# A two-layer hybrid decoder step: key rotation through summed products, earlier lora loads, and new orders in the scan loop and the output projection

## The chip, the cores and the metric

The kernel runs on one core of a Trainium2 chip. Its metric is the device time of one execution in microseconds (us), the median of several runs. The core's engines are TensorE (PE, matrix products into PSUM banks), VectorE (DVE), ScalarE (ACT), GpSimd (POOL) and SyncE (SP, which only issues transfers here). Each engine runs its own list of instructions in the order in which it is written; engines meet only at semaphores.

## The reference

Two groups of tokens share the weights: a prompt of 1024 positions and 8 samples of one position each, so every stage works on T = 1032 columns. Each of two layers does:

```python
h = rmsnorm(x, W['attn_norm'][l])
proj = h @ W['w_in'][l]                       # 1024 -> 2592
q, k = rope(q, positions), rope(k, positions)  # 8 query heads, 2 key heads of 64
yb = swa_banded(q, k, v, sink)                 # or swa_step for the samples: window of 128, learned sinks
w = -softplus(-(w0 + tanh(wlo) @ w_decay_up)) - 0.5 ; decay = exp(-exp(w))
a = sigmoid(a0 + alo @ w_a_up) ; g = sigmoid(glo) @ w_g_up
S = S * decay + (S @ -kk) (kk*a)^T + v k_mod^T ; y = S r     # RWKV-7 scan over 1024 steps
ya = (groupnorm(y) + bonus) * g
x = x + concat(ya, yb) @ W['w_out'][l]
x = x + (silu(h2 @ w_gate) * (h2 @ w_up)) @ w_down,  h2 = rmsnorm(x, ffn_norm)
```

`rope` turns each pair of halves of a head by an angle that grows with the position: x1 cos - x2 sin, x2 cos + x1 sin. All of it is float32, and the states, shifted rows and key and value windows of both groups are outputs too.

## The kernel before, in words

Activations lie features by tokens: 128 features on the partitions, 1032 tokens as three column groups of 344 (`NC3`, `CW`). A projection's weights come in units of 128 x 1024; the products keep float32 accuracy by splitting weight and activation into a high and a low part and summing three matmuls (`column`, L1597 to L1599). So each unit passes three engines ahead of PE: SP loads it (`fill_dma`, L383), ACT rounds it to the high part (`fill_high`, L578), POOL subtracts to get the low part (`fill_low`, L491). There are three slots for units, dealt out by `slot`. One unit and one column group take 24 matmuls, which the text calls a column.

Per layer the stages follow one another: the in-projection; the rotation; windowed attention; attention of the samples; the two loras, decay, and norm of the scan's keys; the scan in 16 chunks of 64 tokens; the output projection `w_out` with the samples' scan step beside it; and the FFN. In the profiled execution layer 0 has them from about 26, 279, 312, 405, 434, 560, 718 and 862 us on, layer 1 begins at 1605 us.

**Rotation.** DVE and PE handle four pairs of query heads, each by column group: PE multiplies by a matrix that swaps the halves (L1632), DVE multiplies the product by the sine table (L1035), the projection by the cosine table (L1036), and adds (L1038); the next pair's product waits for that sum. Then come the keys: for each of two heads and three column groups PE makes two products, of the key rows doubled (L1638) and of the key rows doubled and swapped (L1639), and DVE multiplies and adds them (L1044, L1045, L1047) into `a_k_twice`. Attention's first product (L1674) waits for the last of these.

**Loads.** SP issues the rope tables, mask and windows when the in-projection leaves their memory, and the weights of decay and a (`wda`) and the scan mask (`smask`) after the samples' attention is done (L427, L428). PE's lora product (L1761) waits for both.

**Chunk loop.** Chunk n hands its output, two chunks to a block m of 128 tokens, to a norm over heads: the tables `CENTRE_AT`, `SQUARE_AT` and `NORM_AT` (L317 to L319) say in which chunk block m is centred, squared (ACT, L789), given its root (ACT `y_root`, L794) and normed (DVE, L1289); `tokens_back` (PE, L1904) turns it back. In the first chunks DVE also finishes an elimination for the second half of the chunks (`FIRST`, L1308) and lays out its result (`blocks_out`, `corner_out`) in chunk 5; PE's state product (L1927) waits for DVE's state (L1348).

**w_out.** PE runs columns of the first two column groups, then eight of the third; between them stand the products of the samples' scan step (`dec_sums` L1983 and L1985, `dec_read` L1991, and the norm at L2025 to L2031). Activation blocks 0 to 3 are split here (`out_high` on ACT, L798; `out_low` on POOL, L534), blocks 4 to 7 come back by transfer (L540). `add_out` (DVE, L1431) adds a column to the residual.

**Into the FFN.** While PE runs the third column group, ACT squares the residual, and DVE and ACT make the normed activation's high and low parts of the first two groups (`normed` L1445, `high2` L874, `low2` L1450); the table `NORMED` (L321) says how many of the 16 pairs follow each column. The FFN's first gate product waits for them, and the next for the silu (L883).

## Time and profile before

| what | value |
|---|---|
| median of 3 runs | 3250.84 us (3250.83, 3260.38, 3250.84) |
| profiled execution | 3248.73 us, span 3246.8 us, mean granted clock of PE 0.933 |
| busy PE | 2916.8 us, 90% of the span |
| busy DVE, ACT, POOL | 1461.5, 824.1, 606.3 us |
| chain that ended last | PE 75%, DVE 16%, ACT 4%, issue 3%, DMA 1% |

The page says for each engine how long it worked, and for the chain that ended last which engine held up the end. PE is busy nine tenths of the span, so what can be gained lies in the remaining 330 us, in which PE waits, and in stretches in which its granted clock is half. A row of a timeline gives the start, the duration, the engine, the line, the tile written and those read, and in brackets the idle time before it and what ended that. A row of windows gives busy times in a stretch, then the granted clock (1.00 is 2.4 GHz, 0.50 is 1.2 GHz), the DMA share and the rate.

### The profile page before, as it was taken

To read this page: it belongs to the slowest core of one execution; us is meant where nothing else is said; L and a number is where in the kernel's file an instruction comes from. 1 tells how busy PE (TensorE), PEld (TensorE's weight loads), DVE (VectorE), ACT (ScalarE), POOL (GpSimd) and SP (SyncE) were. 2 spreads that over 40 slices of the span, in tenths; PEclk is the share of its full clock that TensorE was granted. 3 is DMA by queue.
4 is the path that set the end of the run, shared out by engine and by line. 5 is a ranking of instruction groups with operands and counts; after the bars stand their busy time and mean duration, and the time that the engine had idled before them with its cause. 6 is when DMAs were issued, how large, how long until landed. Compare 5 with 4: busy or idle time off the path is not lost.

```text
span 3246.8 us, 49233 instructions
## 1 busy us (share of the span) xinstructions
PE 2916.8 (90%) x20858; PEld 2741.4 (84%) x20858; DVE 1461.5 (45%) x2549; ACT 824.1 (25%) x1727; POOL 606.3 (19%) x295
## 2 busy tenths in 40 slices
PE   6996766988899999999999966589898999999997
PEld 6995635878899999999989946368788999999997
DVE  5334749765622322223453275687645322223324
ACT  3000642441311111111310035424323111111112
POOL 2320001013222122222222100000232222222123
PEclk9998966989999999999999988669899999999998
DMA  3111010023211111111211010000322111111111
GB/s 120 46 33 52 1 40 11 15 67 106 65 55 49 40 52 46 46 46 46 81 58 51 15 52 12 29 11 15 111 84 62 46 40 53 47 51 46 40 53 53
DMA packets 55882, 158.13 MB, mean 49 GB/s; under 512 B 9200, under 2 KB 23536, under 8 KB 54896
## 3 DMA queue, kind: packets, MB, share of 16 engines
q1 hardware_dynamic: 52496, 150.76, 14.8%
q0 software_dynamic: 3168, 4.23, 0.5%
q8 instruction: 166, 2.72, 0.3%
q14 instruction: 52, 0.43, 0.0%
HBM read 137.43 MB, written 17.54 MB: 48 GB/s over the span
## 4 chain that ended last, share of the span: by engine, by line
PE 75%; DVE 16%; ACT 4%; issue 3%; DMA 1%; SPq 0%; POOL 0%; DVEq 0%; ACTq 0%
PE bank L1597 21%; PE bank L1599 20%; PE bank L1598 20%; PE bank L1962 1%; PE bank L1958 1%; PE bank L1938 1%; DVE a_stats L1092 1%; PE bank L1819 1%; PE bank L1853 1%; PE bank L1948 1%; PE bank L1761 1%; DVE act_low L964 1%; DVE c_T L1217 1%; PE bank L1665 1%; DVE c_NT L1215 1%
## 5 line engine op out<-in xcount | busy, mean ns | idle before, releaser
L1597 PE MATMUL bank<-act_high,w_high 128*128 128x344 f32 x3504 | 1139.2, 325 | 49.8 <-POOL w_low L491 34.6
L1599 PE MATMUL bank<-act_high,w_low 128*128 128x344 f32 x3504 | 1129.3, 322 | 0.0
L1598 PE MATMUL bank<-act_low,w_high 128*128 128x344 f32 x3504 | 1129.1, 322 | 0.0
L491 POOL TENSOR_TENSOR w_low<-w_raw,w_high 128x1024 fp32r<-128x1024 f32 x206 | 522.0, 2540 | 1677.0 <-ACT w_high L578 1661.1
L1597 PEld LDWEIGHTS bank<-act_high,w_high 128*128 128x128 f32 x3504 | 668.0, 191 | 59.0 <-POOL w_low L491 39.5
L1598 PEld LDWEIGHTS bank<-act_low,w_high 128*128 128x128 f32 x3504 | 666.3, 190 | 2.6 <-issue 2.1
L1599 PEld LDWEIGHTS bank<-act_high,w_low 128*128 128x128 f32 x3504 | 667.5, 191 | 0.0
L1460 DVE TENSOR_TENSOR f_mid<-f_silu,bank 128x344 f32<-128x344 f32 x132 | 67.7, 513 | 852.9 <-PE bank L1599 849.6
L1557 DVE TENSOR_TENSOR resid<-bank,resid 128x344 f32<-128x344 f32 x528 | 270.6, 516 | 209.5 <-PE bank L1599 209.5
L1597 PE MATMUL bank<-f_mid_high,w_high 128*128 128x344 f32 x1056 | 341.8, 324 | 4.1 <-DVE resid L1557 4.0
L1599 PE MATMUL bank<-f_mid_high,w_low 128*128 128x344 f32 x1056 | 339.6, 322 | 0.0
L1598 PE MATMUL bank<-f_mid_low,w_high 128*128 128x344 f32 x1056 | 337.3, 319 | 0.0
L578 ACT CAST w_high<-w_raw 128x1024 fp32r<-128x1024 f32 x206 | 212.5, 1043 | 489.9 <-PE bank L1599 487.0
L1597 PEld LDWEIGHTS bank<-f_mid_high,w_high 128*128 128x128 f32 x1056 | 198.4, 188 | 10.6 <-DVE resid L1557 10.1
L1599 PEld LDWEIGHTS bank<-f_mid_high,w_low 128*128 128x128 f32 x1056 | 198.8, 188 | 0.0
L1598 PEld LDWEIGHTS bank<-f_mid_low,w_high 128*128 128x128 f32 x1056 | 198.5, 188 | 0.2
L1013 DVE TENSOR_TENSOR proj<-bank,s_rstd 128x344 f32<-128x344 f32 x126 | 64.3, 516 | 292.0 <-PE bank L1599 291.9
L890 ACT CAST f_mid_high<-f_mid 128x344 fp32r<-128x344 f32 x132 | 63.5, 481 | 406.7 <-DVE f_mid L1460 406.7
L883 ACT ACTIVATE f_silu<-bank 128x344 f32<-128x344 f32 x132 | 60.2, 458 | 351.7 <-PE bank L1599 351.7
L628 ACT COPY s_raw_last<-proj 128x9 f32<-128x9 f32 x30 | 6.0, 200 | 279.8 <-DVE proj L1013 279.8
L1254 DVE TENSOR_TENSOR c_gram<-bank,consts 128x512 f32<-128x512 f32 x64 | 41.2, 686 | 69.5 <-PE bank L1819 69.2
L1702 PEld LDWEIGHTS bank<-a_probs_t,a_v_padded 128*128 128x128 f32 x512 | 60.0, 196 | 14.6 <-DVE a_probs_t L1075 10.7
(287 smaller groups left out, 3010.3 us busy)
## 6 DMA issues: line engine op xcount, KB each, us to landing
w_raw<-wts SPq DMA_DIRECT2D x206, 512.0 KB, 3.6
resid<-x SPq DMA_DIRECT2D x4, 1376.0 KB, 10.5
att_keep<-act_low SPq DMA_DIRECT2D x2, 2064.0 KB, 10.2
act_low<-att_keep POOLq DMA_DIRECT2D x6, 688.0 KB, 4.6
x_keep<-resid SPq DMA_DIRECT2D x3, 1376.0 KB, 5.8
o_y<-resid SPq DMA_DIRECT2D x3, 1376.0 KB, 5.7
resid<-x SPq DMA_DIRECT2D x4, 516.0 KB, 7.7
...
```

Source lines behind the costliest of these rows:

```text
L491: eng.tensor_tensor(wl[s][:, :], raw[s][:, :], wh[s][:, :].bitcast(F32), ALU.subtract).then_inc(w_low, 1)
L578: eng.copy(wh[s][:, :], raw[s][:, :]).then_inc(w_high, 1)
L883: a(sil[:, c, :], bank[c][:, 0:CW], ACT.Silu).then_inc(scalar_steps, e.step(f"ff{i}_sil{j}{c}"))
L890: eng.copy(mh[:, j, cs(c)], midf[:, c, :]).then_inc(scalar_steps, e.step(f"ff{i}_high{j}{c}"))
L1013: tt(proj[:, k, cs(c)], bank[3 * (k % 2) + c][:, 0:CW], rstd[:, c, :], ALU.mult).then_inc(vector_steps, e.step(f"win_ev{k}{c}"))
L1254: tt(GM[n % 2][:, h], bank[h][:, :].rearrange("p (k t) -> p k t", k=4), bcast(c_("gram"), 1, 4), ALU.mult).then_inc(vector_steps, e.step(f ...
L1460: tt(midf[:, c, :], sil[:, c, :], bank[3 + c][:, 0:CW], ALU.mult).then_inc(vector_steps, e.step(f"ff{i}_mid{j}{c}"))
L1557: tt(x[:, k, cs(c)], bank[(DOWN_LAST if i == NR - 1 else DOWN)[n % (4 if i == NR - 1 else 2)]][:, 0:CW], x[:, k, cs(c)], ALU.add).then_inc ...
L1597: mm(out, wh[s][:, wcols], act_h, start=start, stop=False)
L1598: mm(out, wh[s][:, wcols], act_l, start=False, stop=False)
L1599: return mm(out, wl[s][:, wcols], act_h, start=False, stop=stop)
L1702: last = mm(bank[6][:, 128 * p:128 * p + 128], v, pT[:, 2 * (2 * p + h) + kt, :], start=(h, kt) == (0, 0), stop=(h, kt) == (1, 1))
```

## The change

Five parts, all in both layers. **Keys:** DVE first multiplies the key rows by cosine and by sine (128 x 1032 each); PE makes both products into one bank, where they are summed (`key_heads`), head 0 after the first query pair and head 1 after the second; ACT copies the six sums to `a_k_twice`. **Loads:** `wda` and `smask` are issued directly behind the value window, and the tiles that share their memory are moved. **Chunk loop:** the centre, square and norm of the first four blocks come one chunk later, the elimination's steps are dealt out anew, its layout is spread over chunks 5 to 7, and the root of block 6 is taken ahead of chunk 15's copy. **w_out:** the first column comes before the samples' sums, the samples' steps come a column or two later, and the first units are loaded and split earlier than the second group's activations. **Into the FFN:** ACT splits the next unit before it squares, `NORMED` deals out the pairs differently with five after the loop, and the second silu comes before the first high part.

```diff
-CENTRE_AT = {6: 0, 7: 1, 8: 2, 9: 3, 11: 4, 12: 5, 14: 6}
-SQUARE_AT = {7: 0, 8: 1, 9: 2, 10: 3, 12: 4, 13: 5, 15: 6}
-NORM_AT = {8: 0, 9: 1, 10: 2, 11: 3, 13: 4, 14: 5}
+CENTRE_AT = {7: 0, 8: 1, 9: 2, 10: 3, 11: 4, 12: 5, 14: 6}
+SQUARE_AT = {8: 0, 9: 1, 10: 2, 11: 3, 12: 4, 13: 5, 15: 6}
+NORM_AT = {9: 0, 10: 1, 11: 2, 12: 3, 13: 4, 14: 5}
-NORMED = (0, 3, 5, 7, 9, 12, 14, 16)
+NORMED = (0, 2, 4, 6, 8, 9, 10, 11)
...
+eng.dma_start(wda, row("wda").rearrange("p (w n) -> p w n", w=2)).then_inc(lora_in, e.load("lora_in"))
+eng.dma_start(smask[:, :], d["smask"]).then_inc(lora_in, e.load("lora_in", "lora_in"))
...
 if l:
     eng.wait_ge(spill, e.at("spill"))
-eng.wait_ge(tensor_steps, e.at(f"y{NCH - 1}"))
+eng.wait_ge(tensor_steps, e.at(f"y{NCH - 2}"))
 eng.sem_inc(sync_idle, 1)
 fill_dma(l, NIN, wait=False)
...
     eng.dma_start(hl[:, 4:8, cs(c)], kept_low[:, :, cs(c)]).then_inc(att_back[c], e.load(f"att_back{c}", f"att_back{c}"))
-    if c < 2:
+    if c == 0:
         for o in range(4):
             out_low(c, o)
 eng.sem_inc(pool_idle, 1)
 fill_low(l, NIN)
+for o in range(4):
+    out_low(1, o)
+eng.wait_ge(vector_steps, e.at("y_n7"))
+fill_low(l, NIN + 1)
 eng.wait_ge(tensor_steps, e.at("yt7"))
-fill_low(l, NIN + 1)
 fill_low(l, NIN + 2)
 for k in range(NIN + 3, UL + 3 if l < L - 1 else UL):
     fill_low(l, k)
-    if k == NIN + 7:
+    if k == NIN + 8:
         for o in range(4):
             out_low(2, o)
...
+eng.wait_ge(pool_steps, e.at("att_zero"))
 for g in range(2):
-    eng.wait_ge(vector_steps, e.at("kd_last"))
+    for c in range(NC3):
+        eng.wait_ge(tensor_steps, e.at(f"rk{g}{c}"))
+        eng.copy(kd[:, g, WIN + c * CW:WIN + (c + 1) * CW], bank[3 + c][:, 0:CW]).then_inc(scalar_steps, e.step(f"kd{g}{c}"))
+for g in range(2):
...
+    if n == NCH - 1:
+        y_root(SQUARE_AT[n])
...
 
-y_square(7)
 eng.wait_ge(vector_steps, e.at("y_gated5"))
+fill_high(l, NIN)
 for o in range(4):
     out_high(1, o)
-fill_high(l, NIN)
+y_square(7)
+eng.wait_ge(state_out, e.at("state_out"))
+fill_high(l, NIN + 1)
 y_root(7)
...
     fill_high(l, NIN + 3 + k, used=f"wo_mm{k}1")
-    if k == 3:
+    if k == 4:
         eng.wait_ge(tensor_steps, e.at("dn_var"))
         a(drs[:, 0:32], bank[2][:, 64:96], ACT.Sqrt, bias=eps_lnx, scale=1.0 / HD).then_inc(scalar_steps, e.step("dn_root"))
-    if k == 4:
+    if k == 5:
         eng.wait_ge(vector_steps, e.at("dn_out"))
         for o in range(4):
...
+    fill_high(l, NIN + KT + 3 + k, used=f"wo_mm{k}2")
     square(k, 2)
-    fill_high(l, NIN + KT + 3 + k, used=f"wo_mm{k}2")
     if k == 0:
         root("n2", 0)
         root("n2", 1)
     else:
         for i in range(NORMED[k - 1], NORMED[k]):
             high2(i // KT, i % KT)
+for i in range(NORMED[-1], 2 * KT):
+    high2(i // KT, i % KT)
 silu(0, 0, 0)
 root("n2", 2)
 for k in range(KT):
     high2(2, k)
+silu(0, 0, 1)
 mid_high(0, 0, 0)
 silu(0, 1, 0)
-silu(0, 0, 1)
 mid_high(0, 0, 1)
 silu(0, 1, 1)
 silu(0, 0, 2)
...
 eng.sem_inc(vector_idle, 1)
+tt(kcos[:, :], proj[:, 19, :], cos[:, :], ALU.mult).then_inc(vector_steps, e.step("k_cos"))
+tt(ksin[:, :], proj[:, 19, :], sin[:, :], ALU.mult).then_inc(vector_steps, e.step("k_sin"))
...
-for g in range(2):
-    for c in range(NC3):
-        kt = kd[:, g, WIN + c * CW:WIN + (c + 1) * CW]
-        eng.wait_ge(tensor_steps, e.at(f"rk{g}{c}"))
-        eng.wait_ge(vector_steps, e.mine())
-        tt(rt[:, c, :], bank[3 + c][:, 0:CW], sin[:, cs(c)], ALU.mult).then_inc(vector_steps, e.step())
-        tt(kt, bank[c][:, 0:CW], cos[:, cs(c)], ALU.mult).then_inc(vector_steps, e.step())
-        eng.wait_ge(vector_steps, e.mine())
-        tt(kt, kt, rt[:, c, :], ALU.add).then_inc(vector_steps, e.step("kd_last" if (g, c) == (1, 2) else f"kd{g}{c}"))
 
...
-FIRST = (0, 0, 5, 8, 13, 16, 21, 24, 29, 31)
+FIRST = (0, 0, 5, 9, 12, 15, 19, 22, 27, 31)
 grams(0)
...
-        for h in range(2):
-            blocks_out(1, h, 1)
-            corner_out(1, h)
+        blocks_out(1, 0, 1)
+    elif n < 8:
+        corner_out(1, 0) if n == 6 else blocks_out(1, 0, 0)
     if n + 1 < NCH:
...
     elif n == 5:
-        for h in range(2):
-            blocks_out(1, h, 0)
+        blocks_out(1, 1, 1)
+    elif n < 8:
+        corner_out(1, 1) if n == 6 else blocks_out(1, 1, 0)
     if n in NORM_AT:
...
+for i in range(NORMED[-1], 2 * KT):
+    if i + 1 < 2 * KT:
+        normed((i + 1) // KT, (i + 1) % KT)
+    low2(i // KT, i % KT)
 inverse("n2", 2)
...
 eng.wait_ge(vector_steps, e.at(f"win_ev{NIN - 1}2"))
+def key_heads(g):
+
+    eng.wait_ge(vector_steps, e.at("k_sin"))
+    for c in range(NC3):
+        if g:
+            eng.wait_ge(scalar_steps, e.at(f"kd0{c}"))
+        mm(bank[3 + c][:, 0:CW], dup[:, 128 * g:128 * g + 128], kcos[:, cs(c)], start=True, stop=False)
+        mm(bank[3 + c][:, 0:CW], rdup[:, 128 * g:128 * g + 128], ksin[:, cs(c)], start=False, stop=True).then_inc(tensor_steps, e.step(f"rk{g}{c}"))
+
 for p in range(4):
+    if p in (1, 2):
+        key_heads(p - 1)
     for c in range(NC3):
         if p:
             eng.wait_ge(vector_steps, e.at(f"rq_add{p - 1}{c}"))
         mm(bank[c][:, 0:CW], rotm, proj[:, 15 + p, cs(c)], start=True, stop=True).then_inc(tensor_steps, e.step(f"rq_rot{p}{c}"))
+eng.wait_ge(scalar_steps, e.at("kd12"))
 eng.wait_ge(vector_steps, e.at("rq_add32"))
-for g in range(2):
-    for c in range(NC3):
-        if g:
-            eng.wait_ge(vector_steps, e.at(f"kd0{c}"))
-        mm(bank[c][:, 0:CW], dup[:, 128 * g:128 * g + 128], proj[:, 19, cs(c)], start=True, stop=True)
-        mm(bank[3 + c][:, 0:CW], rdup[:, 128 * g:128 * g + 128], proj[:, 19, cs(c)], start=True, stop=True).then_inc(tensor_steps, e.step(f"rk{g}{c}"))
-eng.wait_ge(vector_steps, e.at("kd_last"))
 eng.wait_ge(pool_steps, e.at("att_zero"))
...
+out_column(0, 0)
+eng.wait_ge(vector_steps, e.at("y_gated6"))
+tokens_back(7)
 eng.wait_ge(vector_steps, e.at(f"S_new{NCH - 1}"))
 eng.wait_ge(scalar_steps, e.at(f"y_ev{NCH - 1}"))
 dec_sums(0, 0)
-out_column(0, 0)
 dec_sums(0, 1)
-eng.wait_ge(vector_steps, e.at("y_gated6"))
-tokens_back(7)
 out_column(0, 1)
 out_column(1, 0)
+out_column(1, 1)
 dec_read(0)
-out_column(1, 1)
+out_column(2, 0)
 dec_sums(1, 0)
 dec_sums(1, 1)
-out_column(2, 0)
 out_column(2, 1)
+out_column(3, 0)
 dec_read(1)
-out_column(3, 0)
+out_column(3, 1)
+out_column(4, 0)
 eng.wait_ge(vector_steps, e.at("y_gated7"))
 eng.wait_ge(vector_steps, e.at("dec_y11"))
 mm(bank[2][:, 0:32], c_("centre"), dy[:, :], start=True, stop=True).then_inc(tensor_steps, e.step("dn_centred"))
 eng.wait_ge(vector_steps, e.at("dn_r_k_k"))
 mm(bank[2][:, 32:64], bdones, dbp[:, :], start=True, stop=True).then_inc(tensor_steps, e.step("dn_bonus"))
-out_column(3, 1)
+out_column(4, 1)
+out_column(5, 0)
 eng.wait_ge(vector_steps, e.at("dn_squares"))
 eng.wait_ge(vector_steps, e.at("dn_bonus_v"))
 mm(bank[2][:, 64:96], bdones, dsq[:, :], start=True, stop=True).then_inc(tensor_steps, e.step("dn_var"))
-for k in range(4, KT):
+out_column(5, 1)
+for k in range(6, KT):
     out_column(k, 0)
     out_column(k, 1)
 out_column(0, 2)
```

The order of the samples' steps on DVE (from `y_variance(7)` on) follows PE's: column sums come one place earlier, `dec_y`, `dec_squares` and `dec_out` a place or two later.

**Order of instructions.** PE at the rotation of layer 0 before: twelve products of the query pairs, then the keys; `a_rope_mats` holds the matrices, `proj` the projected rows.

```order
1515 L1632 MATMUL bank<-proj,a_rope_mats 128x344 x12
1516 L1638 MATMUL bank<-proj,a_rope_mats 128x344
1517 L1639 MATMUL bank<-proj,a_rope_mats 128x344
1518 L1638 MATMUL bank<-proj,a_rope_mats 128x344
1519 L1639 MATMUL bank<-proj,a_rope_mats 128x344
```

And in the changed kernel, where a piece of three is one query pair:

```order
1515 L1652 MATMUL bank<-proj,a_rope_mats 128x344 x3
1516 L1643 MATMUL bank<-a_k_cos,a_rope_mats 128x344
1517 L1644 MATMUL bank<-a_k_sin,a_rope_mats 128x344
1518 L1643 MATMUL bank<-a_k_cos,a_rope_mats 128x344
...
1522 L1652 MATMUL bank<-proj,a_rope_mats 128x344 x3
1523 L1643 MATMUL bank<-a_k_cos,a_rope_mats 128x344
1524 L1644 MATMUL bank<-a_k_sin,a_rope_mats 128x344
...
1529 L1652 MATMUL bank<-proj,a_rope_mats 128x344 x6
```

The twelve key products moved from behind the query pairs to between them, and read DVE's scaled copies.

POOL at the end of the chunk loop of layer 0 before; a row x4 is `out_low` of one column group, L540 a transfer from `att_keep`, and L491 a unit's low part, from `w_out`'s first on.

```order
41 L540 DMA act_low<-att_keep 128x4x344
42 L534 TENSOR_TENSOR act_low<-proj,act_high 128x344 x4
43 L540 DMA act_low<-att_keep 128x4x344
44 L534 TENSOR_TENSOR act_low<-proj,act_high 128x344 x4
45 L540 DMA act_low<-att_keep 128x4x344
46 L491 TENSOR_TENSOR w_low_63<-w_raw_57,w_high_60 128x1024
47 L491 TENSOR_TENSOR w_low_64<-w_raw_58,w_high_61 128x1024
```

The same place in the changed kernel:

```order
41 L542 DMA act_low<-att_keep 128x4x344
42 L536 TENSOR_TENSOR act_low<-proj,act_high 128x344 x4
43 L542 DMA act_low<-att_keep 128x4x344 x2
44 L493 TENSOR_TENSOR w_low_62<-w_raw_56,w_high_59 128x1024
45 L536 TENSOR_TENSOR act_low<-proj,act_high 128x344 x4
46 L493 TENSOR_TENSOR w_low_63<-w_raw_57,w_high_60 128x1024
47 L493 TENSOR_TENSOR w_low_64<-w_raw_58,w_high_61 128x1024
```

The first unit's low part now stands ahead of the second group's `out_low`.

PE at the start of `w_out` in layer 0 before: `tokens_back` (L1904), the samples' sums on `d_t_a` and `d_t_b`, and the first column's products (L1597 to L1599).

```order
1970 L1904 MATMUL bank<-consts,y_normed_151 128x128 x4
1971 L1983 MATMUL bank<-d_t_a,consts 128x512
1972 L1985 MATMUL bank<-d_t_a,consts 128x512
1973 L1597 MATMUL bank<-act_high,w_high_60 128x344
1974 L1598 MATMUL bank<-act_low,w_high_60 128x344
...
1996 L1599 MATMUL bank<-act_high,w_low_63 128x344
1997 L1983 MATMUL bank<-d_t_b,consts 128x512
1998 L1985 MATMUL bank<-d_t_b,consts 128x512
1999 L1904 MATMUL bank<-consts,y_normed_152 128x128 x4
2000 L1597 MATMUL bank<-act_high,w_high_60 128x344
```

In the changed kernel:

```order
1972 L1918 MATMUL bank<-consts,y_normed_153 128x128 x4
1973 L1606 MATMUL bank<-act_high,w_high_59 128x344
1974 L1607 MATMUL bank<-act_low,w_high_59 128x344
...
1996 L1608 MATMUL bank<-act_high,w_low_62 128x344
1997 L1918 MATMUL bank<-consts,y_normed_154 128x128 x4
1998 L1997 MATMUL bank<-d_t_a,consts 128x512
1999 L1999 MATMUL bank<-d_t_a,consts 128x512
2000 L1997 MATMUL bank<-d_t_b,consts 128x512
2001 L1999 MATMUL bank<-d_t_b,consts 128x512
2002 L1606 MATMUL bank<-act_high,w_high_59 128x344
```

The first column now follows `tokens_back(6)` at once, and both sums stand behind it and behind `tokens_back(7)`.

## Rows read from the trace of the kernel before

**Rows 1.** Page, groups: count, busy us, mean ns, idle before <-releaser.
```profile
L1597 PE MATMUL bank<-act_high,w_high 128*128 128x344 f32 x3504 | 1139.2, 325 | 49.8 <-POOL w_low L491 34.6
L578 ACT CAST w_high<-w_raw 128x1024 fp32r<-128x1024 f32 x206 | 212.5, 1043 | 489.9 <-PE bank L1599 487.0
```

**Rows 2.** Timeline, PE, layer 0: start us, duration us, [idle before <-releaser].
```profile
279.25 4.04 PE L1632 MATMUL bank<-proj,a_rope_mats 128*128 128x344 f32 x8 [7.83 <-DMA a_amask<-amask]
306.81 0.74 PE L1638 MATMUL bank<-proj,a_rope_mats 128*128 128x344 f32 x2
307.39 0.74 PE L1639 MATMUL bank<-proj,a_rope_mats 128*128 128x344 f32 x2
311.72 0.49 PE L1674 MATMUL bank<-a_k_twice,proj 64*128 64x256 f32 x2 [3.58 <-DVE a_k_twice L1047]
```

**Rows 3.** Timeline of DVE in the same stretch, first and last of 36 instructions.
```profile
280.88 0.52 DVE L1035 TENSOR_TENSOR a_rope_tmp<-bank,a_sin 128x344 f32<-128x344 f32 x1 [7.76 <-PE bank L1632]
298.63 0.52 DVE L1038 TENSOR_TENSOR proj<-proj,a_rope_tmp 128x344 f32<-128x344 f32 x1
```

**Rows 4.** Windows: stretch, busy us of PE PEld DVE ACT POOL, clock, DMA.
```profile
284.00:296.00 12.00, 6.71 (x16) 2.32 (x16) 11.48 (x24) 0.00 (x0) 0.00 (x0) 1.00 0.00 0
1888.00:1900.00 12.00, 8.91 (x14) 4.02 (x14) 8.87 (x19) 0.00 (x0) 0.00 (x0) 0.50 0.00 0
```

**Rows 5.** Instructions of one line, 128x1032 products on DVE.
```profile
L1178 DVE TENSOR_TENSOR proj<-proj,e_a_term x8: 1210/1226/1234, 467.1 to 2093.3; 128x1032 f32<-128x1032 f32 x8
```

**Rows 6.** Timeline of PE and ACT, start of the decay stage, layer 0.
```profile
433.96 3.79 PE L1761 MATMUL bank<-proj,e_w_decay_a 64*128 64x512 f32 x8 [6.67 <-DMA e_scan_mask<-smask]
...
427.41 1.06 ACT L704 ACTIVATE proj<-proj 64x1032 f32<-64x1032 f32 x1
```

**Rows 7.** DMA issues while the rope tables load: KB, median us to landing.
```profile
a_v_window<-vwin SPq DMA_DIRECT2D x1, 508.0 KB, 8.1
a_amask<-amask SPq DMA_DIRECT2D x1, 256.0 KB, 6.0
```

**Rows 8.** Timeline of PE, chunk loop of layer 0.
```profile
621.46 0.68 PE L1927 MATMUL bank<-c_S,ar_heads 64*64 64x64 f32 x16 [1.38 <-DVE c_S L1348]
...
642.11 1.07 PE L1938 MATMUL bank<-c_SA,c_Tt 64*64 64x64 f32 x16 [1.16 <-ACT c_SA L812]
```

**Rows 9.** Windows of the chunk loop, layer 0 and layer 1.
```profile
643.00:657.00 14.00, 14.00 (x143) 12.19 (x141) 5.63 (x13) 4.13 (x12) 0.00 (x0) 0.54 0.01 2
2250.00:2262.00 12.00, 11.88 (x189) 10.52 (x190) 8.70 (x19) 6.27 (x18) 0.00 (x0) 1.00 0.00 1
```

**Rows 10.** Timeline of PE, w_out of layer 0.
```profile
721.60 0.69 PE L1904 MATMUL bank<-consts,y_normed 128*128 128x128 f32 x2 [3.48 <-DVE y_normed L1289]
...
724.65 1.19 PE L1983 MATMUL bank<-d_t_a,consts 128*128 128x512 f32 x1 [1.94 <-ACT act_high L798]
...
732.39 0.66 PE L1597 MATMUL bank<-act_high,w_high 128*128 128x344 f32 x1 [3.99 <-POOL w_low L491]
...
775.86 0.38 PE L2025 MATMUL bank<-d_y,consts 128*128 128x32 f32 x2 [3.91 <-DVE d_y L1395]
...
783.59 0.38 PE L2031 MATMUL bank<-d_squares,consts 128*128 128x32 f32 x2 [1.73 <-DVE d_bonus L1411]
```

**Rows 11.** Timeline of ACT at the end of the chunk loop.
```profile
718.15 0.58 ACT L829 COPY y_tokens<-bank 64x512 f32<-64x512 f32 x1 [3.19 <-PE bank L1962]
```

**Rows 12.** Window from w_out's third column to the FFN, layer 0.
```profile
822.00:886.00 64.00, 51.91 (x300) 49.77 (x299) 50.54 (x69) 27.31 (x49) 18.69 (x8) 0.95 0.23 73
```

**Rows 13.** Timeline of PE in the same stretch.
```profile
843.13 0.43 PE L1597 MATMUL bank<-act_high,w_high 128*128 128x344 f32 x1 [2.05 <-POOL w_low L491]
...
849.22 0.42 PE L1597 MATMUL bank<-act_high,w_high 128*128 128x344 f32 x1 [2.05 <-POOL w_low L491]
```

**Rows 14.** Timeline of POOL and of DVE there, one fill.
```profile
827.55 2.40 POOL L491 TENSOR_TENSOR w_low<-w_raw,w_high 128x1024 fp32r<-128x1024 f32 x1 [3.42 <-ACT w_high L578]
...
827.88 2.43 DVE L1450 TENSOR_TENSOR act_low<-n_normed,act_high 128x344 fp32r<-128x344 f32 x1 [1.39 <-ACT act_high L874]
```

More of the change, by code:

```diff
@@ L238, in program @@
         rt = sp("rope_tmp", 3 * CW)[:, :].rearrange("p (c t) -> p c t", c=3)
+        kcos, ksin = (at(f"a_k_{n}", T, RING + 7152 - T * (i + 1)) for i, n in enumerate(("cos", "sin")))
         kro = sp("k_tail", 136)
@@ L289, in program @@
         SA0 = at("c_SA0", 256, RING + 3584)[:, :].rearrange("p (k t) -> p k t", k=4)
-        St = [at(f"c_S{q}", 256, RING + 3840 + 256 * q)[:, :].rearrange("p (k t) -> p k t", k=4) for q in range(2)]
+        St = [at(f"c_S{q}", 256, RING + 4352 - 256 * q)[:, :].rearrange("p (k t) -> p k t", k=4) for q in range(2)]
         elim = [at(f"c_N{f}", 1024, RING + 4608 + 2304 * f) for f in range(2)]
@@ L298, in program @@
         heads_of = lambda v: v.rearrange("p (g i) -> p g i", g=8)
-        yt = [at(f"y_tokens{m}", 512, (PJ + 12 * T + 512 * m, RING + 4608, RING + 7168)[max(m - 2, 0)]) for m in range(5)]
+        yt = [at(f"y_tokens{m}", 512, (PJ + 12 * T + 512 * m, RING + 4608, RING + 6144)[max(m - 2, 0)]) for m in range(5)]
         bv = [at(f"y_bonus_v{m}", 512, (PJ + 12 * T + 1536 + 512 * m, RING + 5120, RING + 5632)[max(m - 2, 0)]) for m in range(5)]
-        lgr = at("y_ln_gain", 512, RING + 6144)
-        ysq = at("y_squares", 512, RING + 6656)
+        lgr = at("y_ln_gain", 512, RING + 7168)
+        ysq = at("y_squares", 512, RING + 7680)
         yn = [at(f"y_normed{q}", 512, RING + 8192 + 512 * q) for q in range(2)]
@@ L348, in program @@
         w_low = sem("w_low_ready")
-        PER_SLOT = (34, 35, 34)
+        PER_SLOT = (35, 34, 34)
         def slot(k):
-            return (k + 2) % 3 if k < NIN else (k - NIN + 1) % 3
+            return (k + 1) % 3 if k < NIN else (k - NIN) % 3
         def unit_of(l, k):
@@ L426, in _ @@
                 eng.wait_ge(k_out, e.at("k_out"))
-                eng.dma_start(wda, row("wda").rearrange("p (w n) -> p w n", w=2)).then_inc(lora_in, e.load("lora_in"))
-                eng.dma_start(smask[:, :], d["smask"]).then_inc(lora_in, e.load("lora_in", "lora_in"))
                 eng.dma_start(d["att_keep"].rearrange("p (k t) -> p k t", k=4).bitcast(F32), hl[:, 4:8, :].bitcast(F32)).then_inc(att_out, e.load("att_out", "att_out"))
@@ L832, in _ @@
                         corner(n + 2, 1, 0)
-                    if n in SQUARE_AT:
+                    if n in SQUARE_AT and n < NCH - 1:
                         y_root(SQUARE_AT[n])
@@ L1473, in _ @@
                 y_variance(7)
+                y_norm(7)
                 dec_in(0, 1)
-                y_norm(7)
+                y_gate(7)
+                add_out(0, 0)
                 dec_back(0, 0)
-                y_gate(7)
                 dec_back(0, 1)
-                add_out(0, 0)
+                add_out(0, 1)
                 dec_state(0)
-                add_out(0, 1)
                 add_out(1, 0)
+                add_out(1, 1)
                 dec_y(0)
+                sum2(1, 0)
                 dec_in(1, 0)
-                add_out(1, 1)
-                sum2(1, 0)
+                add_out(2, 0)
+                sum2(1, 1)
                 dec_in(1, 1)
@@ L1489, in _ @@
                 dec_back(1, 1)
-                add_out(2, 0)
-                sum2(1, 1)
-                dec_state(1)
                 add_out(2, 1)
                 sum2(2, 0)
+                dec_state(1)
                 add_out(3, 0)
```

27 lines of the change are left out of this document (12 added, 15 removed).

## The prediction

> **What bounds the kernel now.** I read the page's groups first, then PE's timeline of each stage that the diff touches, then the windows of those stages. The table of the profile shows PE busy for 2916.8 of 3246.8 us; what the change can give lies in the 330 us without a matmul and in stretches at half clock. The groups say where weights are late: the first of each three products waited 49.8 us in all, 34.6 of it for POOL's low part, while ACT's rounding of a unit takes 1.04 us [rows 1]. The timelines then show that the five edited places hold waits of other kinds: DVE's chain in the rotation, a transfer ahead of the lora product, single stalls in the chunk loop, and in `w_out` and behind it a supply chain of ACT, POOL and DVE. I go through them in the order of a layer, count layer 0 and double it, since layer 1 has the same waits.
>
> **Rotation.** Before, PE may start at 279.25, when the mask has landed [rows 2], and DVE's 36 instructions for the queries run from 280.88 to 298.63 + 0.52 = 299.15 [rows 3], 18.27 us without a gap. Only then come the keys; attention starts at 311.72 [rows 2]. So the keys cost 311.72 - 299.15 = 12.6 us of pure path. After, DVE first makes two products of 128 x 1032. A row of that shape and operation has a median of 1.226 us [rows 5], so they last from 279.35 to 281.8; the queries' chain starts 281.8 - 280.88 = 0.9 us later than before and, if PE keeps up, ends at 300.1. PE gets 6 key products behind the first pair and 6 behind the second. At full clock one follows the next after 307.39 - 306.81 = 0.58 us [rows 2], so six take 3.5 us, against 18.27 / 4 = 4.57 us that DVE spends on a pair: hidden. At half clock six take 7.0 us and DVE waits. The first six start at about 281.8, just behind a DMA wait of 7.83 us [rows 2], and will be cold in part; I give that 1.0 us, so attention starts at about 301.2 and the term is 311.7 - 301.2 = **10.5 us**. ACT's six copies hide behind the third and fourth pair, since ACT has nothing else there (0.00 busy in both windows [rows 4]). Bounds: 11.5 us with no cold product; at half clock all the way PE needs 24 products x 1.16 = 27.8 us from 279.25, and one DVE step of 1.5 us behind, 308.6, which leaves 3.1 us.
>
> **Loads of the lora stage.** PE's product at 433.96 stood 6.67 us for the scan mask; the other thing it needs, ACT's tanh, was done at 427.41 + 1.06 = 428.47 [rows 6]. With the transfers issued some 150 us earlier the tanh is last, and the gain is 433.96 - 428.47 = **5.5 us**. What is moved: two transfers go into the burst of the rope tables. They stand behind the value window in SP's queue, and in this burst what was issued first landed first: the mask after 6.0 us, the value window after 8.1 [rows 7]. So I charge the rotation nothing. If the engines mixed them, two more transfers, each like a window, would delay the mask by up to the 2.1 us between those rows; the term is then 3.4. The Trainium skill ("DMA: Bandwidth & Descriptors", section "Two DMAs through the same engine are not ordered") says that nothing orders transfers across the sixteen engines, which speaks for that lower figure; the landing times of this trace stand against it, without excluding it.
>
> **Chunk loop.** One stall goes with the spread of the elimination's layout: 1.38 us on DVE's state at 621.46 [rows 8]. The other, 1.16 us at 642.11 behind ACT, belongs to the first root and moves a chunk on. The new tables move work between chunks but add none. I take **1.3 us**, bounds 5 (layer 0's half-clock stretch behind 642.11 disappears, below) and -5 (another one appears).
>
> **w_out.** Up to the first column PE waited 3.48 + 1.94 + 3.99 = 9.41 us, and for the samples' norm 3.91 + 1.73 = 5.64 [rows 10]; these five are 15.05 us per layer. After: the loop's last matmul ends at 721.60 - 3.48 = 718.12. ACT's last copy ends at 718.15 + 0.58 = 718.73 [rows 11]; the first unit has been loaded a chunk earlier and is now rounded at once, 1.04 us, to 719.8, and POOL's part takes 2.40 [rows 14], to 722.2. `tokens_back(6)` (724.65 - 1.94 - 721.60 = 1.1 us [rows 10]) fits before that, as block 6's root no longer waits for that copy. So the first column starts at 722.2 and not at 732.39; of 4.1 us, 1.1 are work and 3.0 are waiting: 9.4 - 3.0 = **6.4 us**. `dec_sums` then stands behind the column, where ACT's and DVE's steps have passed. What is queued behind POOL's fill now is the second group's `out_low`; its column comes after two sums and `tokens_back(7)`, at about 733, and the low part is ready at 722.2 + 5.3 = 727.5. For the samples' norm a column or two more stand ahead of each wait. The row at 849.22 less its wait of 2.05, minus 843.13, gives 4.0 us for a column [rows 13], enough for 3.91 and 1.73 if DVE's chain ran unchanged; but additions to the residual now stand ahead of it, so I take three quarters, **4.1 us**. Together **10.5**; bounds 13 (all but the 3.0, and the first column warm) and 5 (the norm's waits stay).
>
> **Into the FFN.** From 822 to 886 PE works 51.91 of 64 us [rows 12]: 12.1 us of waits, two of them of 2.05 us on POOL at 843.13 and 849.22 [rows 13]. ACT now rounds the next unit before it squares, so POOL starts earlier; five pairs are left until after the loop and then stand ahead of the silu. I take half, **6 us**, bounds 11 and 0. Against more speaks a row: DVE's subtraction `low2` beside POOL's fill took 2.43 us, where an operation of that size takes 0.52 elsewhere, and they ended one just behind the other, at 829.95 and 830.31 [rows 3, 14]. The Trainium skill ("SBUF — State Buffer", "Who interferes with whom") has a rule for this: a VectorE operation with two inputs in SBUF and a GpSimd operation that reads SBUF exclude one another for the whole instruction. The rows agree. By it a fill may cost DVE 1.9 us at each of eight columns however the pairs are dealt out, and this term is nothing; the second rival prices that.
>
> **Sum.** 10.5 + 5.5 + 1.3 + 10.5 + 6 = 33.8 us per layer, 67.6 in two. The profiled execution took 3248.7 us and comes to 3181; the median of the runs lies 2.1 us above it, so I say 3183.
>
> **Rivals.**
> First, the rotation is bound by PE at half clock. For it: in layer 1 the clock is 0.50 from 1888 to 1900, though in layer 0 the same work ran at 1.00 from 284 to 296 [rows 4], and the change begins with a wait for DVE. Against: PE has twice the work between the pairs. The term is 3.1 in place of 10.5, 15 us in two layers: 3198.
> Second, supply stays the bound: DVE and POOL exclude one another as above. `w_out` gives 5 and the FFN's start 0, so 2 x 11.5 = 23 us are missing: 3206. For it: the subtraction of 2.43 us [rows 14]. Against: the first column's 6.4 us do not depend on it.
> Third, supply comes free: the FFN's start gives 11 and `w_out` 12.5, 2 x 7 = 14 us more: 3169.
> Fourth, slower: the reordered chunk loop lets PE fall to half clock. The price: behind the stall of 1.16 us [rows 8] layer 0 ran 143 instructions in 14.0 us at 0.54; in layer 1 a stretch of the same loop took 12 us for 189 at 1.00 [rows 9]. Each such stretch costs 14.0 x (1 - (12.0 / 189) / (14.0 / 143)) = 4.9 us. It decides from (67.6 + 10) / 4.9 = 16 stretches on, one in half of the 32 chunks: 3260 and more. Against: the tables remove a stall and create no longer one that I can see, and layer 1 kept its clock.
>
> **How the numbers follow.** Forecast 0.52, first rival 0.13, second 0.16, third 0.12, fourth 0.07. A measurement of this kernel tells about 0.3% from no change, 10 us; all cases but the fourth lie beyond it. Of the fourth I put 0.04 beyond 3260 and 0.02 within 10 us of before. So: faster 0.94, same 0.02, slower 0.04. The range: at the low end third rival with the rotation at its bound, 2 x (11.5 + 5.5 + 3 + 12.5 + 11) = 87, 3164, and a little for the clock: 3158. At the high end the second rival with the first in one layer, 3206 + 7 = 3213, rounded down to 3212, since both at once are rare.
>
> **What would show it.** The rotation: attention's first product about 21.9 us after the first query product, not 32.5, and no DVE instruction on `a_k_twice`. Loads: the lora product released by ACT, not by DMA. Chunk loop: no stall over a microsecond on `c_S`. `w_out`: its first column 4 to 5 us after the loop's last matmul, and no wait near 4 us on POOL or `d_y`. FFN's start: waits of 6 us instead of 12 from the third columns to the first silu. Wrong it would be if the granted clock in the rotation or the loop is 0.50 for most of the stage, or if the third columns keep a period above 6 us.

## The result and the profile after

The changed kernel takes 3167.41 us (median of 4 runs, 3166.18 to 3170.12), the kernel before 3253.82 (4 runs, 3250.83 to 3260.38): a ratio of 0.9733, 95% interval 0.9715 to 0.9751. The profiled execution took 3167.29 us, 81.4 less than that of before, with a mean granted clock of 0.945 instead of 0.933. The forecast was 3183, so the direction was right and the gain larger than its sum. The page's head and its first group after:

```profile
span 3165.3 us, 49209 instructions
PE 2885.1 (91%) x20858; PEld 2722.5 (86%) x20858; DVE 1453.9 (46%) x2517; ACT 830.3 (26%) x1739; POOL 613.3 (19%) x295
L1606 PE MATMUL bank<-act_high,w_high 128*128 128x344 f32 x3504 | 1134.7, 324 | 42.5 <-POOL w_low L493 24.3
```

PE is busy 31.7 us less for the same 20858 matmuls: that part of the gain is not waiting, but matmuls of which fewer run at half clock. The group answers to [rows 1]: 10.3 us less wait on POOL's low part.

Where it went, as differences between two starts on PE's timeline, kernel before minus kernel after:

| stage | forecast per layer | layer 0 | layer 1 |
|---|---|---|---|
| first query product to attention's first | 10.5 | 9.8 | 10.0 |
| to the lora product | 5.5 | 4.1 | 3.8 |
| to the loop's first products with the state | 0 | -1.5 | 0.0 |
| to the loop's last matmul | 1.3 | 7.2 | 13.4 |
| to the third columns' first sum of squares | 10.5 | 13.7 | 11.9 |
| to the FFN's first down product | 6 | 3.2 | 4.2 |
| sum | 33.8 | 36.4 | 43.4 |

The third row shows no effect of the change: over all profiles of this case that stage takes between 131.1 and 134.0 us.

**Rotation.** PE's timeline of layer 0 (start, duration, what it read, idle time before):

```profile
278.23 3.81 PE L1652 MATMUL bank<-proj,a_rope_mats 128*128 128x344 f32 x6 [7.46 <-DMA a_amask<-amask]
282.61 0.74 PE L1644 MATMUL bank<-a_k_sin,a_rope_mats 128*128 128x344 f32 x2
283.19 0.74 PE L1643 MATMUL bank<-a_k_cos,a_rope_mats 128*128 128x344 f32 x2
285.50 1.90 PE L1652 MATMUL bank<-proj,a_rope_mats 128*128 128x344 f32 x6
290.70 1.90 PE L1652 MATMUL bank<-proj,a_rope_mats 128*128 128x344 f32 x6
300.92 1.65 PE L1688 MATMUL bank<-a_k_twice,proj 64*128 64x256 f32 x6 [3.25 <-issue]
```

The key products follow one another after 0.58 us, as in [rows 2], and attention starts 22.7 us after the first query product; forecast 21.9, before 32.5. On DVE the second of the scaled copies, and the two waits of the chain for a query product that stands behind six key products:

```profile
279.48 1.23 DVE L1043 TENSOR_TENSOR a_k_sin<-proj,a_sin 128x1032 f32<-128x1032 f32 x1
286.35 0.52 DVE L1049 TENSOR_TENSOR a_rope_tmp<-bank,a_sin 128x344 f32<-128x344 f32 x1 [1.07 <-PE bank L1652]
291.55 0.52 DVE L1049 TENSOR_TENSOR a_rope_tmp<-bank,a_sin 128x344 f32<-128x344 f32 x1 [0.67 <-PE bank L1652]
```

1.23 us a copy and the first wait of 1.07 us were worked out as 1.226 and 1.0. The second wait, 0.67 us, was not: one pair's query products and the six key products behind them take PE 290.70 - 285.50 = 5.20 us at full clock, and DVE's pair takes 4.57.

**Loads.** The lora product, answering to [rows 6]:

```profile
419.03 1.22 PE L1775 MATMUL bank<-proj,e_w_decay_a 64*128 64x512 f32 x2 [1.28 <-DVE e_heads_r_k L1150]
```

No transfer releases it any more. The releaser named had ended at 418.63; ACT's tanh ended at 417.87 + 1.06 = 418.93. In the DMA issues of the burst the two new transfers do not delay the mask, which lands after 5.6 us ([rows 7]: 6.0), and they themselves land last:

```profile
e_w_decay_a<-wda SPq DMA_DIRECT2D x1, 512.0 KB, 8.3
a_amask<-amask SPq DMA_DIRECT2D x1, 256.0 KB, 5.6
```

**Chunk loop.** Windows from one new state to the next (length, then busy times of PE, its loads, DVE, ACT and POOL with counts, granted clock, DMA). First chunk 9 of layer 0 and chunk 1 of layer 1 before:

```profile
646.69:662.43 15.74, 15.74 (x177) 13.92 (x178) 7.34 (x16) 4.74 (x13) 0.00 (x0) 0.65 0.01 1
2172.05:2186.55 14.50, 14.50 (x143) 12.88 (x142) 6.50 (x21) 3.29 (x9) 0.00 (x0) 0.50 0.01 2
```

And after, chunk 1 and the chunk that now holds the stall of 1.16 us ([rows 8] had it a chunk earlier):

```profile
560.22:567.94 7.72, 7.72 (x137) 6.97 (x136) 7.13 (x22) 3.94 (x11) 0.00 (x0) 1.00 0.01 2
629.14:640.37 11.23, 10.07 (x165) 8.91 (x163) 6.21 (x12) 6.16 (x15) 0.00 (x0) 1.00 0.01 1
```

All fifteen intervals of both layers have a clock of 1.00, and from first to last new state they take 134.94 and 134.96 us, against 142.09 and 146.68 before. The stall of 1.38 us on `c_S` is gone; the one of 1.16 us is not, and is no longer followed by half clock. The shortest chunks of the two layers before, put together, make 136.4: only 1.5 us per layer come from the order itself, close to the 1.3 of the forecast; the rest is clock.

**w_out and into the FFN.** PE's waits, answering to [rows 10] and [rows 13]:

```profile
698.46 0.66 PE L1918 MATMUL bank<-consts,y_normed 128*128 128x128 f32 x4 [0.91 <-DVE y_normed L1294]
701.99 0.62 PE L1606 MATMUL bank<-act_high,w_high 128*128 128x344 f32 x1 [2.87 <-POOL w_low L493]
744.96 1.13 PE L2005 MATMUL bank<-d_t_a,consts 128*128 128x512 f32 x2 [2.51 <-DVE d_t_a L1392]
815.22 0.42 PE L1606 MATMUL bank<-act_high,w_high 128*128 128x344 f32 x1 [1.44 <-DVE resid L1436]
823.62 0.66 PE L1606 MATMUL bank<-act_high,w_high 128*128 128x344 f32 x1 [4.37 <-DVE resid L1436]
```

The first column starts 4.4 us after the loop's last matmul (forecast 4.1, before 14.3) and the waits on `d_y` and `d_squares` are gone. Before the FFN no column waits on POOL now, but PE waits 4.37 us for an addition to the residual. DVE and POOL at that time show why:

```profile
817.86 2.71 DVE L1450 SCALAR_TENSOR_TENSOR n_normed<-resid,params,s_rstd 128x344 f32<-128x344 f32 x1
820.49 2.65 DVE L1455 TENSOR_TENSOR act_low<-n_normed,act_high 128x344 fp32r<-128x344 f32 x1
823.06 0.50 DVE L1436 TENSOR_TENSOR resid<-bank,resid 128x344 f32<-128x344 f32 x1
```

```profile
817.57 5.19 POOL L493 TENSOR_TENSOR w_low<-w_raw,w_high 128x1024 fp32r<-128x1024 f32 x2 [3.63 <-ACT w_high L583]
```

POOL splits two units back to back; beside the first a product of DVE takes 2.71 us and beside the second a subtraction 2.65, and the addition that PE needs is queued behind both.

### The profile page after: what moved, and what is told of

It reads as the page before. It is cut to its first block, busy times and chain, and to the rows that moved or that the text cites. A ratio compares the mean times of both kernels' runs of the same rounds, so it can differ in the third digit from the quotient of the medians.

```text
span 3165.3 us, 49209 instructions
## 1 busy us (share of the span) xinstructions
PE 2885.1 (91%) x20858; PEld 2722.5 (86%) x20858; DVE 1453.9 (46%) x2517; ACT 830.3 (26%) x1739; POOL 613.3 (19%) x295
## 4 chain that ended last, share of the span: by engine, by line
PE 77%; DVE 15%; ACT 4%; issue 3%; DMA 1%; SPq 0%; DVEq 0%; POOL 0%; ACTq 0%
PE bank L1606 21%; PE bank L1608 21%; PE bank L1607 21%; PE bank L1976 1%; PE bank L1972 1%; DVE a_stats L1097 1%; PE bank L1867 1%; PE bank L1952 1%; PE bank L1962 1%; PE bank L1833 1%; PE bank L1775 1%; DVE n_square_sum L1443 1%; DVE act_low L1455 1%; DVE c_T L1222 1%; DVE c_NT L1220 1%
## 5 line engine op out<-in xcount | busy, mean ns | idle before, releaser
L493 POOL TENSOR_TENSOR w_low<-w_raw,w_high 128x1024 fp32r<-128x1024 f32 x206 | 529.6, 2577 | 1670.0 <-ACT w_high L583 1665.8
L1606 PEld LDWEIGHTS bank<-f_mid_high,w_high 128*128 128x128 f32 x1056 | 198.1, 188 | 10.7 <-DVE resid L1566 10.1
L1716 PEld LDWEIGHTS bank<-a_probs_t,a_v_padded 128*128 128x128 f32 x512 | 61.6, 201 | 14.6 <-DVE a_probs_t L1080 10.7
L1716 PE MATMUL bank<-a_probs_t,a_v_padded 128*128 128x128 f32 x512 | 64.2, 286 | 9.3 <-DVE a_probs_t L1080 6.2
```

The source lines that it names most:

```text
L493: eng.tensor_tensor(wl[s][:, :], raw[s][:, :], wh[s][:, :].bitcast(F32), ALU.subtract).then_inc(w_low, 1)
L1606: mm(out, wh[s][:, wcols], act_h, start=start, stop=False)
L1716: last = mm(bank[6][:, 128 * p:128 * p + 128], v, pT[:, 2 * (2 * p + h) + kt, :], start=(h, kt) == (0, 0), stop=(h, kt) == (1, 1))
```

## Experiments

Twelve runs follow: ten edited kernels, one of them twice, and the kernel before again. Code is shortened to what tells the edit. Differences are between medians and the 3167.4 us of the changed kernel, unless before is named. The changed kernel was timed in one session only; the kernel before, timed anew beside each group of runs, had medians of 3248.4 to 3255.5 us, so a difference of medians under some 5 us shows little, and stage times decide. These are again differences of starts on PE.

**Rotation undone.** The key products and DVE's 18 instructions stand behind the queries again:

```diff
-    if p in (1, 2):
-        key_heads(p - 1)
+for g in range(2):
+    for c in range(NC3):
+        mm(bank[c][:, 0:CW], dup[...], proj[:, 19, cs(c)], start=True, stop=True)
+        mm(bank[3 + c][:, 0:CW], rdup[...], proj[:, 19, cs(c)], start=True, stop=True)
```

> The changed kernel with the rotation as before: DVE rotates the keys behind the queries. Base 3167.4 us. Theory (gains add up by stage): the rotation stage is 9.8 us longer in layer 0 and 10.0 in layer 1, so 3187 us, between 3185 and 3190, and the chunk loop keeps its 134.9 us per layer at a granted clock of 1.00. Rival (the loop's half-clock stretches depend on when the loop is reached, not on its order): a stretch below 1.00 comes back in a loop that is reached 10 us later, which makes it 5 to 11 us longer, 3192 to 3200 us.

3187.21 us (3184.11 to 3189.64), plus 19.8. The stage is 10.4 and 9.7 us longer, both loops stay at 1.00 with 135.0 us: the rival falls, the stage's term holds. In the profiled run the next stage, attention, is 1.9 and 1.2 us shorter, so a little of the gain is given back there: in the changed kernel attention begins at half clock (below).

**Loads undone.**

```diff
-eng.dma_start(wda, ...)     # behind the value window
-eng.dma_start(smask, ...)
+eng.dma_start(wda, ...)     # behind the samples' attention
+eng.dma_start(smask, ...)
```

> The changed kernel with the decay weights and the scan mask issued late again. Theory (wait of the transfer): the lora product waits 6.7 us for the mask again instead of 1.3, plus 5.4 us per layer, 3178 us (3176 to 3180). Rival (given back by a half clock behind the earlier start): only 2 to 3.5 us per layer are lost, 3171 to 3175 us.

3186.37 us (3179.0 to 3190.71), plus 19.0, above both expectations. Its profiled run was the lowest, 3179.0, 11.7 more than the profiled run of the changed kernel: there the wait is back, and the stage up to the lora product is 4.7 and 5.2 us longer.

```profile
424.39 1.22 PE L1775 MATMUL bank<-proj,e_w_decay_a 64*128 64x512 f32 x2 [6.84 <-DMA e_scan_mask<-smask]
```

**Loads undone, a second look**, the same kernel.

> The changed kernel with the late loads once more, for a second profile, since its four times lay between 3179.0 and 3190.7 us and the profiled one was the lowest. If the dearer runs begin their chunk loop at half clock, a run near 3190 us shows a first chunk of 14.5 us at 0.50 in one or both layers instead of 7.7 at 1.00. If not, the loop is as in the first profile and the difference lies in the rotation or in attention.

3180.09 us, and the profile is like the first: first chunks of 7.8 us at 1.00 in both layers, the stage 5.2 and 5.4 us longer. So 12 us are shown. The up to 11 more of its dearer runs were in no profile, but those runs have a mean granted clock of 0.940 against 0.944 in the first profile. By that difference they spend some 25 us more at half clock (0.004 x 3188 / 0.5, an estimate), and a stretch at half clock costs up to half its length, so they can hold the 11 us. In which stage stays open.

**Loop undone.**

```diff
-CENTRE_AT = {7: 0, 8: 1, 9: 2, 10: 3, 11: 4, 12: 5, 14: 6}
+CENTRE_AT = {6: 0, 7: 1, 8: 2, 9: 3, 11: 4, 12: 5, 14: 6}
-FIRST = (0, 0, 5, 9, 12, 15, 19, 22, 27, 31)
+FIRST = (0, 0, 5, 8, 13, 16, 21, 24, 29, 31)
...
-    if n == NCH - 1:
-        y_root(SQUARE_AT[n])
```

> The changed kernel with the tables of the chunk loop, the parts of the elimination and the place of the root as before. Theory A (the order of the loop keeps PE's clock up): half-clock stretches return, the loop takes 142 to 147 us per layer instead of 134.9, 3180 to 3190 us. Theory B (the stretches of the kernel before were set by when the loop is reached, or by chance, and the tables are worth only the stall on the state): the loop stays at a granted clock of 1.00 and takes about 136.4 us, 3169 to 3172 us.

3184.54 us (3183.45 to 3186.26), plus 17.1. Windows of the same chunk in layer 0 and layer 1:

```profile
634.07:644.54 10.47, 10.47 (x168) 9.21 (x167) 7.34 (x17) 4.83 (x13) 0.00 (x0) 1.00 0.01 2
2200.77:2216.63 15.86, 15.86 (x180) 14.03 (x180) 7.34 (x17) 4.75 (x13) 0.00 (x0) 0.66 0.01 2
```

The loops take 136.95 and 141.94 us: in one layer what theory B said, in the other a stretch at half clock. Theory A holds for the middle of the loop, though not in every pass. The edit takes back the tables, the elimination's parts and the root together; which of the first two keeps the clock up was not tried. The other part of the 17.1 us is a wait that I had booked under `w_out`: without the early root the block's turn waits 6.23 us instead of 0.91, and the first column comes 2.6 us later after the loop.

```profile
708.44 0.90 PE L1917 MATMUL bank<-consts,y_normed 128*128 128x128 f32 x3 [6.23 <-DVE y_normed L1294]
```

**Loop alone**: the same edit the other way, on the kernel before.

> The kernel before with the new tables of the chunk loop, the new parts of the elimination and the earlier root, nothing else. Base 3250.8 us. Theory A (the order keeps the clock up): the loop takes about 135 us in both layers at a granted clock of 1.00, 7 and 12 us less, 3232 us. Theory B (arrival or chance): 1.5 us less per layer and a stretch at half clock in at least one layer, 3243 to 3249 us.

3230.68 us (3220.82 to 3230.89); before beside it 3255.03 (ratio 0.9911, 0.9892 to 0.9929). Layer 0's loop takes 135.02 us at 1.00. In layer 1 it takes 143.28, because the first chunk ran at half clock, while the middle kept 1.00:

```profile
2160.76:2175.27 14.51, 14.51 (x143) 12.89 (x142) 7.26 (x23) 3.29 (x9) 0.00 (x0) 0.50 0.01 2
2238.01:2249.24 11.23, 10.06 (x165) 8.91 (x163) 6.21 (x13) 6.16 (x15) 0.00 (x0) 1.00 0.01 1
```

So the two half-clock stretches of before are different things: the new order ends the one in the middle, and by itself not the one at the entry.

**The kernel before again**, for a second profile.

> The kernel before, unchanged, for a second profile. If the half-clock stretches of its chunk loop are fixed by the program, they stand at the same chunks again (chunk 9 of layer 0, chunk 1 of layer 1) and the loop takes 142.1 and 146.7 us between the first and the last new state. If they come by chance, they stand elsewhere or are missing, and the sum of both loops differs by 5 us or more. Time 3251 to 3260 us either way.

3254.45 us (3239.68 to 3264.52, 10 runs); the profiled one took 3260.13. The loops again take 146.68 and 142.09 us, but with the layers exchanged: the slow first chunk is in layer 0 and the slow middle in layer 1.

```profile
575.43:589.93 14.50, 14.50 (x142) 12.88 (x142) 6.50 (x21) 3.29 (x9) 0.00 (x0) 0.50 0.01 1
2258.58:2274.30 15.72, 15.72 (x177) 13.91 (x178) 7.33 (x16) 4.76 (x13) 0.00 (x0) 0.65 0.01 2
```

Neither is bound to a layer. Over all profiles: with the old order 2 of 6 loops entered at half clock, and of the 4 others 3 fell in the middle; with the new order 1 of 22 entered at half clock and none fell in the middle.

The entry sorts by something else, by what stands ahead of the loop. Behind the earlier stages of before, 3 of 6 loops entered at half clock (one in each profile of before, one in that of the loop alone). Behind the changed stages, with at most one part undone, none of 22 did, two of them with the old order of the loop. So the change seems to end this stretch too, by its earlier parts; no run tells by which.

**First column undone**: PE's order alone.

```diff
 tokens_back(6)
-out_column(0, 0)
-tokens_back(7)
 dec_sums(0, 0)
+out_column(0, 0)
 dec_sums(0, 1)
+tokens_back(7)
```

> The changed kernel with PE's order at the start of the output projection as before: the samples' first sums ahead of the first column, the second sums and the last block's turn behind it; loads, ACT, POOL and DVE stay as changed. Theory (PE's order carries the 6.4 us of the forecast): the first column starts 5 to 7 us later per layer, 3178 to 3181 us. Rival (the supply, changed on SP, ACT and POOL, carries it, and the sums only fill its wait): plus 0 to 2 us per layer, 3167 to 3171 us.

3170.28 us (3167.56 to 3172.25), plus 2.9: the rival. The first column starts 7.9 us after the loop's last matmul instead of 4.4, but the sums are done by then; they stand in the waiting time.

```profile
704.19 2.04 PE L1997 MATMUL bank<-d_t_a,consts 128*128 128x512 f32 x2 [3.52 <-DVE d_t_a L1370]
```

So little of the first column's gain rests on PE's order. The earlier root moves it by 2.6 us, undone as well as alone (11.7 us after the loop's last matmul instead of 14.3); the rest must be the earlier loading and splitting of the first units, which no run undid.

**Samples' norm undone**; DVE's and ACT's steps move back too, only PE's are shown.

```diff
-out_column(3, 1)
-out_column(4, 0)
 mm(bank[2][:, 0:32], c_("centre"), dy[:, :], ...)
 mm(bank[2][:, 32:64], bdones, dbp[:, :], ...)
-out_column(4, 1)
-out_column(5, 0)
+out_column(3, 1)
 mm(bank[2][:, 64:96], bdones, dsq[:, :], ...)
```

> The changed kernel with the samples' steps behind the second sums at their old places on PE, DVE and ACT. Theory: the waits of 3.9 us for d_y and 1.7 us for d_squares return, plus 4 to 6 us per layer, 3175 to 3179 us. Rival (DVE's additions, which now start earlier, leave room for the chain at the old places): plus 0 to 2 us per layer, 3167 to 3171 us.

3181.23 us (3180.66 to 3181.43), plus 13.8, 6.1 us per layer in this stage: the theory. Both waits are back at their old length:

```profile
749.15 0.38 PE L2040 MATMUL bank<-d_y,consts 128*128 128x32 f32 x2 [3.91 <-DVE d_y L1401]
756.87 0.38 PE L2046 MATMUL bank<-d_squares,consts 128*128 128x32 f32 x2 [1.73 <-DVE d_bonus L1417]
```

**FFN's start undone.**

```diff
-NORMED = (0, 2, 4, 6, 8, 9, 10, 11)
+NORMED = (0, 3, 5, 7, 9, 12, 14, 16)
-    fill_high(l, NIN + KT + 3 + k, used=f"wo_mm{k}2")
     square(k, 2)
+    fill_high(l, NIN + KT + 3 + k, used=f"wo_mm{k}2")
```

> The changed kernel with the old table of pairs, squares ahead of the weights' high part, and the second silu behind the first high part. Theory (the part is worth what its stage shows): third columns to the first silu take 63.4 us again instead of 58.7 and 64.4 instead of 58.7, so plus 10.4 us, 3178 us. Rival (the gain of that stage comes from the earlier arrival of the squares and additions, not from the order here): 3167 to 3171 us.

3180.96 us (3179.79 to 3182.57), plus 13.6: the theory. The stage is 4.8 us longer in both layers. The one before it is 1.6 longer, but not by this edit: the 1.6 us are a stretch at half clock behind the wait of 2.5 us for `d_t_a`, before the third columns, and **Two fills later** and layer 0 of **Loads undone** have the same.

Windows of the 10 us from that wait's end, in the changed kernel and in this one:

```profile
744.96:754.96 10.00, 10.00 (x58) 9.04 (x59) 5.40 (x12) 1.93 (x3) 2.10 (x1) 1.00 0.14 49
```

```profile
746.10:756.10 10.00, 10.00 (x46) 8.76 (x47) 5.10 (x11) 1.92 (x3) 0.50 (x1) 0.83 0.16 52
```

**GpSimd reads nothing in the third columns.** Eight low parts per layer are left out and replaced by zeros:

```diff
-eng.tensor_tensor(wl[s][:, :], raw[s][:, :], wh[s][:, :].bitcast(F32), ALU.subtract).then_inc(w_low, 1)
+eng.memset(wl[s][:, :].bitcast(F32), 0.0).then_inc(w_low, 1)   # NIN + KT + 3 <= k < FF0 + 3
```

> The changed kernel, but the low parts of the eight units rounded during the third columns (units 3 to 7 of the output projection's second pass and the FFN's first three) are left out: GpSimd fills the tile with zeros, which reads nothing, instead of subtracting. Base 3167.4 us. Theory (the two engines exclude one another): DVE's products and sums of 2.4 to 2.7 us in this stretch fall to 0.5 to 0.6, the waits of 1.4 and 4.4 us on the residual's addition go, minus 4 to 6 us per layer, 3155 to 3160 us. Rival (the stretch is bound by DVE's own work or by the supply of units): 3164 to 3168 us.

3150.01 us (3145.81 to 3151.55), minus 17.4, more than expected. From the sum of squares to the first down product it takes 77.4 us instead of 88.1 and 88.0, 10.7 less per layer. POOL's fill and a DVE product beside it:

```profile
811.00 0.96 POOL L494 MEMSET w_low<- 128x1024 f32 x1 [2.82 <-ACT w_high L586]
```

```profile
811.20 0.57 DVE L1453 SCALAR_TENSOR_TENSOR n_normed<-resid,params,s_rstd 128x344 f32<-128x344 f32 x1
```

The product runs at its 0.57 us within the fill, and no wait of PE on the residual is left; the next is 0.52 us for the silu, at 822.21. PE's waits on the residual and the silu in this stage account for 6.5 of the 10.7 us, the rest goes with the stretches at half clock behind them. The fill is also 1.4 us shorter, so the 10.7 us per layer are the price of both, but PE waited on DVE there and not on POOL.

**Two fills later**, to keep them from DVE's last pairs.

```diff
+    if k < 6:
         fill_high(l, NIN + KT + 3 + k, used=f"wo_mm{k}2")
...
+fill_high(l, FF0 + 1, used="wo_mm62")
 silu(0, 0, 0)
 root("n2", 2)
+fill_high(l, FF0 + 2, used="wo_mm72")
```

> The changed kernel with the last two of those units rounded later: the FFN's second unit behind the five pairs that are left over, the third behind the root of the third group. GpSimd then subtracts while DVE waits for that root. Theory (exclusion): the pair of 2.71 and 2.65 us at the last column takes 1.1, the wait of 4.4 us on the residual's addition shrinks to about 0.5, the silu comes some 3 us earlier, 3159 to 3163 us. Rival (the time comes back as a later unit or a later root, since ScalarE rounds in front of the silu and GpSimd meets DVE's third group): 3166 to 3170 us.

3183.13 us (3182.45 to 3183.82), plus 15.7: the rival, and more of it. DVE's last pairs took 0.5 us, but PE needs the FFN's second unit sooner than I had assumed:

```profile
833.44 0.62 PE L1609 MATMUL bank<-act_high,w_high 128*128 128x344 f32 x1 [10.21 <-POOL w_low L493]
```

**One fill later**, the FFN's third unit alone.

> The changed kernel with only the FFN's third unit rounded later, behind the root of the third group. Theory (exclusion): one of the two operations of 2.7 us at the last column falls to 0.5, minus 2 us per layer, 3162 to 3164 us. Rival (given back in the third group's pairs): 3166 to 3169 us.

3172.28 us (3170.32 to 3172.86), plus 4.9: the wait on the residual at the last column falls from 4.37 to 2.20 us, and 8.47 us on POOL's low part come in place of that and of the 1.21 and 2.07 us that PE waited for the silu. No version of full precision beat the changed kernel.

## Why the prediction was right, and where its sum was off

The direction was right, and the waits named in four of the five places went or shrank as said: 67.6 us forecast, 81.4 between the profiled runs. Most of the difference is the loop, 20.6 us in two layers and not 2.6; the other four terms measured 61 and not 65.

- **Rotation**, 10.5 forecast, 9.8 and 10.0 measured. Copies and the first wait of about 1 us came as worked out. The hiding did not quite: I set six key products (3.5 us) against DVE's 4.57 us for a pair and left out the pair's own query products on PE, with which a turn takes 5.20. The second wait, 0.67 us, is what the term falls short by. Of the first rival nothing is seen within this stage, but attention behind it now begins at half clock.
- **Loads**, 5.5 forecast. The wait fell by 5.4 us as computed and the burst charged nothing, but attention took 1.3 and 1.6 us more (in layer 0 its first 7 us ran at a clock of 0.63 instead of 0.77), so that stage shows 4.1 and 3.8. This is the rotation's price: with the rotation undone attention is 1.9 and 1.2 us shorter again. Undoing the loads costs 6 us per layer in both its profiles.
- **Chunk loop**, 1.3 forecast, 7.2 and 13.4 measured. This is the term that was mis-sized. The order is worth 1.5 us, as forecast; I had left the half-clock stretch of 14 us in the bounds as if it were chance. It is not: with the old order it came in three of four loops entered at full clock, with the new in none of 21, at 5 us each. And I had counted layer 0 and doubled it. Layer 1 had not kept its clock, though I wrote so against the fourth rival: its first chunk ran at half clock, 14.5 us instead of 7.0. That is why its 13.4 us lie so far beyond the bound of 5. The prediction had no term for that, and which part of the change ends it is open. The fourth rival had the mechanism and price right (4.9 us a stretch forecast, 5.3 measured) and the sign wrong.
- **w_out**, 10.5 forecast, 13.7 and 11.9 measured. Against the second profile of before it is 16.8 and 17.1, so the stage of before itself varies by up to 5 us. The samples' norm is worth 6.1, all of its 5.64 of waits and a little more, and not the three quarters that I took (which would be 4.2, not 4.1): nothing in DVE's new queue delayed it. The first column came when computed, but 2.6 us of that are the root ahead of the last copy, and PE's order, which I named beside it, is worth 2.9 us in two layers; that the supply brought the rest is argued and not shown.
- **Into the FFN**, 6 forecast, 3.2 and 4.2 measured; undone, 4.8 in both layers. POOL's waits went as said, but half of 12.1 us was a guess, and PE's waits of 1.44 and 4.37 us on DVE came in their place. The second rival's mechanism is what limits the term: zeros in place of the subtraction free 10.7 us per layer. It did not cost `w_out` what that rival said.

The third rival's time, 3169, lies nearest to the result, but for another reason: supply did not come free, the clock did.
